# Spreading the twelve early down products over twelve pairs of the dense expert loop

## The reference, cut to what matters

```python
def block(args):
    hb, eb, gb = args                          # a block of 128 tokens
    u = jnp.take(expert_down, eb, axis=0)
    act = jax.nn.gelu(jnp.einsum('td,thkd->thk', hb, u))
    wv = (gb * act).astype(expert_up.dtype)
    vv = jnp.take(expert_up, eb, axis=0)
    return jnp.einsum('thk,thkd->td', wv, vv)
```

## Time and profile before

| what | us |
|---|---|
| median of three runs | 2777.44 (2773.61 to 2780.27) |
| the profiled execution | 2776.76 |
| its span | 2774.9 |
| PE busy in the span | 2695.9 (97%) |
| DVE busy | 2211.4 (80%) |
| POOL busy | 1987.4 (72%) |
| ACT busy | 885.0 (32%) |

### The profile page before, as it was taken

One profiled execution on the slowest core, in us unless ns is written; L12 is line 12 of the kernel. 1 busy time (PEld: TensorE's weight loads), 2 busy tenths in 40 slices (PEclk: granted clock), 3 DMA queues, 4 the chain that ended last, 5 costly groups with the idle time before them and its releaser, 6 DMA issues.

```text
span 2774.9 us, 40216 instructions
## 1 busy us (share of the span) xinstructions
PE 2695.9 (97%) x14885; PEld 2375.2 (86%) x14885; DVE 2211.4 (80%) x4772; ACT 885.0 (32%) x1511; POOL 1987.4 (72%) x1505
## 2 busy tenths in 40 slices
PE   8999999999998999999999999999999999999997
PEld 6688787787898998899989988998899889988996
DVE  2522788653998968888889998888999988889998
ACT  4422444324324652222222223222222322222222
POOL 5543578585886877777777867776877688768774
PEclk9999999999999999999999999999999999999999
DMA  4133422224234999999989989998999899989995
GB/s 158 62 92 106 160 69 92 76 84 146 78 104 173 291 299 329 336 352 341 346 329 337 357 320 346 341 346 313 345 351 332 318 362 352 344 308 361 339 348 204
DMA packets 267730, 717.78 MB, mean 259 GB/s; under 512 B 20880, under 2 KB 104208, under 8 KB 267536
## 3 DMA queue, kind: packets, MB, share of 16 engines
q0 software_dynamic: 110912, 403.75, 38.6%
q1 hardware_dynamic: 156624, 311.48, 33.4%
HBM read 657.73 MB, written 57.41 MB: 258 GB/s over the span
## 4 chain that ended last, share of the span: by engine, by line
PE 44%; DVE 8%; DMA 6%; POOL 4%; issue 1%; ACT 1%; SPq 0%; DVEq 0%; ACTq 0%
PE abank L1914 8%; PE abank L1916 7%; PE abank L1915 7%; PE ybank L1930 7%; PE ybank L1931 7%; PE ybank L1929 7%; DMA up<-in_down,e_idx 3%; DVE acc L2091 2%; DMA up<-in_up,e_idx 2%; DVE up L2079 2%; POOL tdown_lo L1861 1%; DVE e_y L2165 1%; POOL up L1854 1%; DMA w<-all_pre 1%; POOL tup_lo L1865 1%
## 5 line engine op out<-in xcount | busy, mean ns | idle before, releaser
L1914 PE MATMUL abank<-m_hT,tdown_hi 128*128 128x384 f32 (+1 forms) x1856 | 578.2, 312 | 13.9 <-DVE w_lo L2157 9.5
L1916 PE MATMUL abank<-m_hT,tdown_lo 128*128 128x384 f32 (+1 forms) x1856 | 577.3, 311 | 0.0
L1915 PE MATMUL abank<-m_hlo,tdown_hi 128*128 128x384 f32 (+1 forms) x1856 | 576.4, 311 | 0.0
L2091 DVE SCALAR_TENSOR_TENSOR acc<-up,e_act,acc 128x1024 f32<-128x1024 f32 x381 | 489.6, 1285 | 68.0 <-DMA up<-in_up,e_idx 49.9
L2079 DVE CUSTOM_DVE_ANT_0 up<-up,acc 128x1024 f32<-128x1024 f32 x384 | 455.5, 1216 | 89.7 <-DMA up<-in_down,e_idx 89.0
L1929 PE MATMUL ybank<-tup_hi,w_hi 128*128 128x512 f32 x1280 | 502.7, 393 | 12.7 <-DVE w_lo L2157 10.2
L1001 POOL TENSOR_TENSOR m_wlo<-m_raw,m_whi 128x1024 fp32r<-128x1024 f32 x128 | 311.5, 2437 | 273.4 <-ACT m_whi L772 269.5
L1930 PE MATMUL ybank<-tup_lo,w_hi 128*128 128x512 f32 x1280 | 501.6, 392 | 0.0
L1931 PE MATMUL ybank<-tup_hi,w_lo 128*128 128x512 f32 x1280 | 501.0, 391 | 0.0
L1854 POOL DMA_INDIRECT up<-in_down,e_idx x384 | 363.2, 946 | 99.5 <-issue 83.9
L1854 POOL DMA_INDIRECT up<-in_up,e_idx x384 | 362.3, 943 | 99.2 <-issue 77.3
(11 more groups left out here) (279 smaller groups left out, 4178.0 us busy)
## 6 DMA issues: line engine op xcount, KB each, us to landing
e_tup<-in_up SPq DMA_DIRECT2D x128, 512.0 KB, 5.3
m_raw<-in_tiles SPq DMA_DIRECT2D x116, 512.0 KB, 3.5
e_tdown<-in_downT SPq DMA_DIRECT2D x116, 512.0 KB, 5.4
gates<-all_table SPq DMA_DIRECT2D x64, 640.0 KB, 4.2
all_table<-t_out SPq DMA_DIRECT2D x9, 4096.0 KB, 14.7
m_raw<-in_downT SPq DMA_DIRECT2D x12, 512.0 KB, 3.7
up<-in_down,e_idx POOLq DMA_INDIRECT x384, 6.6
up<-in_up,e_idx POOLq DMA_INDIRECT x384, 6.5
```

Source lines behind the costliest of these rows:

```text
L1914: nc.tensor.matmul(out, tdown_hi[:, q, at], h2T_hi[:, k, a:b], start=k == 0, stop=False)
L1915: nc.tensor.matmul(out, tdown_hi[:, q, at], h2T_lo[:, a:b, at], start=False, stop=False)
L1916: ins = nc.tensor.matmul(out, tdown_lo[:, q, at], h2T_hi[:, k, a:b], start=False, stop=k == KD - 1)
L2091: ins = nc.vector.scalar_tensor_tensor(out=acc[:], in0=src, scalar=act_of[:, b, k:k + 1], in1=acc[:], op0=ALU.mult, op1=ALU.add)
```

## The change

Twelve pairs, 4, 9, ..., 59, now have one early tile each, q = 1; their tile 0 is computed in the loop like any other. The functions that count finished products (`normal`, `normal_of`, `halves_of`) follow. `load_pre` now takes the number i of the early product, the buffer of `w` is i % 2, and the load stands at the head of SP's round instead of at its end. In `SHARE`, doubled so as to stay whole, the pair before an early tile has 13 of 20, which is 8 or 9 rows.

```diff
-PRE = list(range(4, NPAIR, 10))
-NPRE = 2 * len(PRE)
+PRE = [(p, 1) for p in range(4, NPAIR, 5)]
+NPRE = len(PRE)
...
-                src = io["tiles"][i] if g < NG else io["downT"][2 * PRE[i // 2] + i % 2]
+                src = io["tiles"][i] if g < NG else io["downT"][2 * PRE[i][0] + PRE[i][1]]
...
-SHARE = [3 if p + 1 in PRE or p + 1 == NPAIR else 10 if p else 6 for p in range(NPAIR)]
+SHARE = [13 if (p + 1, 1) in PRE else 6 if p + 1 == NPAIR else 20 if p else 12 for p in range(NPAIR)]
...
-def normal(p):
+def normal(p, q=0):
-    return p - sum(n < p for n in PRE)
+    return 2 * p + q - sum(n < (p, q) for n in PRE)
+def normal_of(p, q):
+    return p - sum(n < p and of == q for n, of in PRE)
+def halves_of(n, half=1):
+    return 2 * n + half + 1
...
             def load_tdown(p, q):
-                if p in PRE:
+                if (p, q) in PRE:
                     return
-                sp.wait_ge(down_low, 2 * (normal(p) - 1) + q + 1)
+                before = max(n for n in range(p) if (n, q) not in PRE)
+                sp.wait_ge(down_low, normal(before, q) + 1)
...
-            def load_pre(p, q):
-                read = PRE.index(p) and PRE[PRE.index(p) - 1]
-                sp.wait_ge(gl_ready if read else w_low, halves(read, q))
-                sp.dma_start(w[:, q], scr["pre"][2 * PRE.index(p) + q]).then_inc(pre_in[q], 16)
+            def load_pre(i):
+                if i >= 2:
+                    sp.wait_ge(gl_ready, halves(*PRE[i - 2]))
+                else:
+                    sp.wait_ge(w_low, halves(0, i % 2))
+                sp.dma_start(w[:, i % 2], scr["pre"][i]).then_inc(pre_in[i % 2], 16)
...
             for p in range(NPAIR):
+                if (p + 2, 1) in PRE:
+                    load_pre(PRE.index((p + 2, 1)))
                 if p + 2 < NPAIR:
                     load_tdown(p + 2, 1)
...
-                if p + 2 in PRE:
-                    for q in range(2):
-                        load_pre(p + 2, q)
...
             def down_rest(p, q):
-                if p in PRE:
+                if (p, q) in PRE:
                     return
-                pool.wait_ge(down_high, 2 * normal(p) + q + 1)
+                pool.wait_ge(down_high, normal(p, q) + 1)
...
             def down_high_of(p, q):
-                if p in PRE:
+                if (p, q) in PRE:
                     return
-                act.wait_ge(tdown_in[q], 16 * (normal(p) + 1))
+                act.wait_ge(tdown_in[q], 16 * (normal_of(p, q) + 1))
                 if p:
-                    act.wait_ge(a_ready, halves(normal(p) - 1, q))
+                    before = max(n for n in range(p) if (n, q) not in PRE)
+                    act.wait_ge(a_ready, halves_of(normal(before, q)))
...
             def expert_gelu(p, q, half):
-                if p in PRE:
+                if (p, q) in PRE:
+                    i = PRE.index((p, q))
                     if half == 0:
-                        act.wait_ge(pre_in[q], 16 * (PRE.index(p) + 1))
+                        act.wait_ge(pre_in[i % 2], 16 * (i // 2 + 1))
                     act.wait_ge(w_low, halves(p, q, half) - 2)
-                    src = w[:, q, cols]
+                    src = w[:, i % 2, cols]
                 else:
-                    act.wait_ge(a_ready, halves(normal(p), q, half))
+                    act.wait_ge(a_ready, halves_of(normal(p, q), half))
```

More of the change, by code:

```diff
@@ L1900, in down_half @@
             def down_half(p, q, half):
-                if p in PRE:
+                if (p, q) in PRE:
                     return
                 if half == 0:
-                    pe.wait_ge(down_low, 2 * normal(p) + q + 1)
+                    pe.wait_ge(down_low, normal(p, q) + 1)
                 if (p, q) == (0, 1) or (p, q) == (1, 0):
@@ L2048, in _ @@
             junk = [tdown[:, 0], tdown[:, 1], tup[:, 0], tup[:, 1], h2[:]]
-            act.wait_ge(down_low, 2 * normal(NPAIR))
+            act.wait_ge(down_low, normal(NPAIR))
             act.wait_ge(up_low, 2 * NPAIR)
```

## The result

The change makes the kernel slower: 2818.4 us (median of 4 runs, 2812.97 to 2819.18) against 2778.8 us, a ratio of 1.0144 with a 95% interval from 1.0133 to 1.0156. The profiled execution took 2819.18 us with a span of 2817.3 us, 42.4 us more than before.

A forecast was written before the change was run, and what follows sets the result against it. PE was taken as the bound, busy 97%, losing 31.2 us in the loop. Twelve short rounds at 5.2 (62.4) plus 4.6 for handovers make 67.0 lost instead, +35.8 us: 2812 us, range 2790 to 2828.

The forecast's parts named there:

- The row of part f: DVE's row, first gathered behind POOL's `down_rest(p + 2, 0)`, makes PE's up 4 stall 3.7 us in each short round.
- The clock: In each short round the granted clock falls after PE's stall: 1.4 us per stall, between 0 and 1.65.
- POOL leaves the short round late: POOL ends 1.6 us into the next round, 1 late; that round has 3 us in hand and loses nothing.
- The loads at the head of SyncE's round: Loads of `w` move past those of `tdown`, `tup` and `gates`; ACT's 18.3 us of waits go, with POOL's lateness.
- The handovers: At row-block changes: 0.7 and 2.1 us in rounds 11 and 21, about 0.7 and 1.1 in 22 and 32; 4.6 together.
- B: Gathers land at the trace's fastest, 4.1 us; stall 2.0 us, no clock fall; no change, 2776 us; chance 0.07.
- Rival A: Up 4 waits only for DVE's own pace, 0.8 us, not for row f; faster, 2761 us; chance 0.10.

The follow-up runs named there:

- experiment 2: Changed kernel with DVE's part f empty in the twelve short rounds, its rows moved to part g behind `add_y(p, 2)`: 2781.4 us, ratio 1.0015.
- experiment 3: Changed kernel with POOL issuing part d of its gathers ahead of `down_rest(p + 2, 0)` in the short rounds: 2763.74 us, ratio 0.9953.
- experiment 1: Changed kernel with a share of 10 instead of 13 for the short rounds, 6 or 7 rows instead of 8 or 9: 2819.49 us, ratio 1.014.
- experiment 5: Changed kernel with PE computing the second bank of up piece 3 three times in short rounds: 2797.28 us, ratio 1.0082.
- experiment 6: Kernel with tile 1 alone early and part d ahead, loads put back last: 2757.23 us; also the kernel before with loads first: 2771.29 us.

## Why the prediction was right

The prediction was right in sign, in mechanism and in size: 2812 (its own sum gives 2813) in a range of 2790 to 2828, measured 2818.4; 36 us more than before were forecast, 40 measured. The mean of a stall was met, its spread from round to round was not. Step by step:

- **The row of part f.** Shown. The chain stands in round 53 as it was worked out from round 16: gather at 11.25 forecast, 11.24 measured; gather to row 5.7, measured 5.78; up 4 at 18.8 to 18.9, measured 18.96. Over the twelve rounds the time that up 4 comes too late is 42.9 us, 3.6 each, against 3.7. But the bounds of 3.3 to 4.3 held in only seven of them: it is 2.6 to 3.0 us in rounds 8, 13, 28 and 33 and 5.2 in round 43. The gather is issued at 11.25 to 11.35 in all twelve, and what differs is its way to DVE: 4.6 to 4.9 us in those four, 7.2 in round 43, 5.7 to 5.9 in the others, 5.6 in the mean. Why was not looked into. Experiments 2 and 3 take the wait away from either end, and experiment 1 excludes the amount of rows.
- **The clock.** Forecast 1.4 us a round, with bounds 0 and 1.65. In the trace the twelve rounds lose 20.9 us beyond the waits, of which some 1.1 are restarts (0.09 in each of rounds 13 and 33, which kept their clock), and so 1.6 to 1.7 us a round go to the clock; experiment 5 gives 18 us back with one fall left. The term was too small by 0.2 to 0.3 us, because in four rounds the slow stretch was twice as long as the one in the trace of before, and those lost 2.6 to 2.8 us, above the upper bound. Two waits, 2.47 and 2.79 us by the trace, brought no fall. That such waits slow PE each time, as the Trainium skill says in "TensorE: Matmul & The Clock Gate", section "HAM oscillation — how this bites in real kernels", holds here for ten of twelve. That one figure for all twelve came out near is in part luck, as it is a mean of rounds that lose nothing, about 1.6 and about 2.7 us.
- **POOL leaves the short round late, and it costs nothing.** Right: the rounds behind lose 0.7 us in all, as the stall and the slow clock make the short round longer and POOL catches up in it. In experiment 2 there is no stall, and the rounds behind lose 17.8 us.
- **The loads at the head of SyncE's round.** ACT's waits for them went, as forecast, but not by their new place: with them last, in experiment 6, ACT does not wait either.
- **The handovers.** Forecast 4.6, measured 7.1 (rounds 21, 22, 32 and 42 by 2.1, 0.9, 1.4 and 2.8; round 11 nothing). Round 42 was not in the sum: before, it took 27.05 us with a down half less at its end, and I had expected what it loses to fit into a full round of 27.89.
- **What was not foreseen.** The loop starts 3.0 us later (1049.5 instead of 1046.5) and its round 0 is 1.1 shorter. Other variants started at 1044.8, so I take this for spread of the stages ahead of it.

The sum: 63.8 + 7.1 + 0.7 is 71.6 us lost instead of 31.2, with 2.0 for the start 42.4 us, which is the difference of the spans.

Of the rivals, B came in part. Its landing of 4.1 us never came to the row of part f, but in four rounds it was near. In round 13, for one, 4.60 us lie between the gather and the read, PE waited 2.47 us, and the clock held:

```profile
1414.85 0.96 POOL L1866 DMA_INDIRECT up<-in_up,e_idx  x1
...
1419.45 1.29 DVE L2105 SCALAR_TENSOR_TENSOR acc<-up,e_act,acc 128x1024 f32<-128x1024 f32 x1 [1.81 <-DMA up<-in_up,e_idx]
```

Of all gathers of the loop the fastest landed in 4.2 us, with a median of 6.3. The estimate of 3.2 us from "DMA: Bandwidth & Descriptors" in the Trainium skill, section "Anatomy of one DMA — SWDGE (gpsimd) path", is too low for these gathers. Rival A had the right price for the wrong case: 2761 was forecast for a kernel in which nothing waits for row f, and experiment 3, which makes just that, gave 2763.74.

## What to carry to other kernels

When work is cut from an engine that is the bound, look at every place where it meets the others: a chain that starts behind an earlier piece of that engine and comes back through three other queues does not get shorter, and what had 3 us in hand is then late by the cut less those 3 us (here 7.1 us were cut, and up 4 was 3.6 us late). Follow the row by its number through both orders, that of the engine that issues and that of the one that consumes; here one row was first behind a wait in one list and last ahead of an addition in the other. And an idle spell on another engine (5.4 us of POOL) marks the place where the work that comes too late could have been put.

## What the runs showed that was not expected

The twelve waits of PE for 2.5 to 5.0 us cost, taken together, nearly half as much again by the clock. Twelve matmuls per short round that compute nothing new made the kernel some 18 us faster, as they kept the granted clock at full speed. Of the waits over 2 us in the loop of the changed kernel ten had a fall of the clock inside or just behind them and two not, and their lengths overlap (2.47 and 2.79 without, 2.65 and 2.69 with one); what decides between them stays open.
